# A hybrid encoder layer on one core: gelu and add of the hidden experts slot by slot in the prompt's merge, in place of pairs

## The reference, cut to what matters

```python
# the merge, for each group of tokens
gates = sigmoid(h @ w_gate + b_gate); ga, gb = split(gates)
merged = ga * (oa @ w_oa) + gb * (ob @ w_ob)
x = x + merged @ w_out
# the experts: idx and g hold 8 heads x 16 slots for each token
u, v = expert_u[idx], expert_v[idx]
act = gelu(einsum('chkd,cd->chk', u, xc))          # one dot product a slot
out = einsum('chk,chkd->cd', g * act, v)           # one scaled add a slot
```

## Time and profile before

| what | value |
|---|---|
| time, median of 3 runs | 4975.61 us (4974.44 to 4983.41) |
| the profiled execution | 4982.06 us, its span 4980.1 us |
| TensorE matmul busy | 3114.3 us, 63% of the span |
| VectorE busy | 3330.1 us, 67% |
| ScalarE busy | 1035.4 us, 21% |
| GpSimd busy | 1748.6 us, 35% |
| mean granted clock of TensorE | 0.738 of full speed |
| mean rate of all transfers | 315 GB/s |

### The profile page before, as it was taken

One profiled execution on the slowest core, in us unless ns is written; L12 is line 12 of the kernel. 1 busy time (PEld: TensorE's weight loads), 2 busy tenths in 40 slices (PEclk: granted clock), 3 DMA queues, 4 the chain that ended last, 5 costly groups with the idle time before them and its releaser, 6 DMA issues.

```text
span 4980.1 us, 72192 instructions
## 1 busy us (share of the span) xinstructions
PE 3114.3 (63%) x27052; PEld 1785.4 (36%) x27052; DVE 3330.1 (67%) x7712; ACT 1035.4 (21%) x2821; POOL 1748.6 (35%) x1393
## 2 busy tenths in 40 slices
PE   7686489885999989954545445455455454454333
PEld 6545367664777744431312212122122122121000
DVE  4426777786888845558867767667667667577554
ACT  3311111221555511111121121111111211111111
POOL 0200033224434233314444444444444444444443
PEclk9897699987999999975656656566666566665555
DMA  6142388896444386679999999999999999999998
GB/s 237 62 165 108 105 323 323 341 338 258 167 176 164 148 304 249 244 289 383 392 399 386 389 402 393 390 408 383 397 400 395 407 386 389 387 397 389 395 398 333
DMA packets 281851, 1568.76 MB, mean 315 GB/s; under 512 B 28064, under 2 KB 48032, under 8 KB 112928
## 3 DMA queue, kind: packets, MB, share of 16 engines
q0 software_dynamic: 184320, 1342.26, 68.6%
q1 hardware_dynamic: 97184, 221.90, 12.0%
HBM read 1510.52 MB, written 53.53 MB: 314 GB/s over the span
## 4 chain that ended last, share of the span: by engine, by line
DMA 31%; PE 7%; issue 7%; DVE 5%; POOL 4%; ACT 2%; another core or an unknown queue 0%; POOLq 0%; DVEq 0%; SPq 0%; ACTq 0%
DMA prompt_exp_ring<-in_experts_dram,prompt_exp_idx 28%; PE prompt_exp_acc L1966 6%; POOL prompt_exp_ring L1619 4%; DVE prompt_exp_junk L1864 3%; DMA prompt_exp_ring<-in_experts_dram,prompt_exp_idx_all 3%; ACT prompt_exp_diag L1696 2%; PE prompt_exp_qp L1927 1%; DVE prompt_exp_pos L1743 0%; DVE prompt_exp_best L1739 0%; PE prompt_exp_qp L1987 0%; DVE prompt_exp_dot L1864 0%; DMA prompt_exp_wq<-in_w_query_dram 0%; DVE prompt_exp_crest L1748 0%; DVE prompt_exp_topi L1743 0%
## 5 line engine op out<-in xcount | busy, mean ns | idle before, releaser
L1966 PE MATMUL prompt_exp_acc<-prompt_exp_ring,prompt_exp_diag 32*32 32x512 f32 x16384 | 939.8, 944 | 1400.8 <-ACT prompt_exp_diag L1696 1397.3
L1864 DVE CUSTOM_DVE_ANT_0 prompt_exp_junk<-prompt_exp_ring,prompt_exp_h_now 128x1024 bf16<-128x1024 f32 x1024 | 1244.6, 1227 | 703.3 <-DMA prompt_exp_ring<-in_experts_dram,prompt_exp_idx 661.0
L1619 POOL DMA_INDIRECT prompt_exp_ring<-in_experts_dram,prompt_exp_idx x896 | 1032.2, 1152 | 1378.0 <-PE prompt_exp_acc L1966 1212.4
L1966 PEld LDWEIGHTS prompt_exp_acc<-prompt_exp_ring,prompt_exp_diag 32*32 32x32 f32 x16384 | 169.7, 127 | 1953.7 <-issue 1951.1
L1690 ACT ACTIVATE prompt_exp_ge<-prompt_exp_dot 128x2 f32<-128x2 f32 x512 | 104.2, 203 | 2291.1 <-DVE prompt_exp_dot L1864 2291.0
L144 POOL DMA_INDIRECT bg_ring<-in_experts_dram,bg_idx x128 | 176.8, 1381 | 663.4 <-DVE bg_acc L180 363.9
L1927 PEld LDWEIGHTS prompt_exp_qp<-prompt_exp_hT,prompt_exp_wq 128*128 128x128 f32 x2048 | 309.9, 240 | 146.3 <-issue 143.2
L283 POOL DMA_INDIRECT sample_hid_ring<-in_experts_dram,sample_hid_idx x128 | 149.5, 1168 | 549.9 <-DVE sample_hid_acc L313 527.8
L1927 PE MATMUL prompt_exp_qp<-prompt_exp_hT,prompt_exp_wq 128*128 128x128 f32 x2048 | 332.9, 330 | 4.5 <-DMA prompt_exp_wq<-in_w_query_dram 2.6
L296 DVE CUSTOM_DVE_ANT_0 sample_hid_junk<-sample_hid_ring,sample_hid_h 128x1024 bf16<-128x1024 f32 x128 | 203.6, 1591 | 155.5 <-DMA sample_hid_ring<-in_experts_dram,sample_hid_idx 145.6
L703 PE MATMUL prompt_proj_acc<-prompt_proj_w_hi,prompt_proj_hT_hi 128*128 128x512 f32 x640 | 261.1, 408 | 25.7 <-ACT prompt_proj_w_hi L596 21.8
(11 more groups left out here) (349 smaller groups left out, 5050.2 us busy)
## 6 DMA issues: line engine op xcount, KB each, us to landing
sample_proj_w<-in_w_all_dram SPq DMA_DIRECT2D x10, 2048.0 KB, 9.3
prompt_proj_w<-in_w_all_dram SPq DMA_DIRECT2D x10, 2048.0 KB
proj_dram<-prompt_proj_stage SPq DMA_DIRECT2D x80, 256.0 KB
prompt_exp_ring<-in_experts_dram,prompt_exp_idx POOLq DMA_INDIRECT x896
sample_exp_wq<-in_w_query_dram SPq DMA_DIRECT2D x4, 2048.0 KB, 15.4
prompt_att_q<-proj_dram SPq DMA_DIRECT2D x16, 512.0 KB
mixed_dram<-prompt_att_OT SPq DMA_DIRECT2D x8, 1024.0 KB, 3.8
prompt_mrg_mixT<-mixed_dram SPq DMA_DIRECT2D x8, 1024.0 KB
```

What stands on the lines that cost most here:

```text
L1619: nc.gpsimd.indirect_dma_start(out=ring[:, s % RING, :], out_offset=None, in_=experts, in_offset=bass.IndirectOffsetOnAxis(ap=column(s), a ...
L1864: nc.vector.tensor_tensor_reduce(out=junk[:, s % 2, :], in0=ring[:, s % RING, 0:D], in1=h_now[:], scale=1.0, scalar=0.0, op0=ALU.mult, op1 ...
L1966: last = nc.tensor.matmul(acc[at:at + Q, rows, :], diag[k, (g - 1) % 2, c, :], ring[k, s % RING, D + half * 512:D + half * 512 + 512], sta ...
```

## The change

One number: the plan of the merge has groups of one slot in place of two. The lag stays one group.

```diff
         PLACES = 6
-        plan = Plan(first, SLOTS - first, PLACES * G, 2, 1)
+        plan = Plan(first, SLOTS - first, PLACES * G, 1, 1)
```

## The result

| | before | after |
|---|---|---|
| median of four runs | 4976.56 us (4974.44 to 4983.41) | 4946.55 us (4939.81 to 4952.47) |
| ratio | | 0.9934, 95% interval 0.9912 to 0.9955 |
| the profiled execution | 4982.06 us, span 4980.1 | 4939.81 us, span 4937.9 |
| VectorE busy | 3330.1 us | 3340.8 us |
| ScalarE busy | 1035.4 us | 1042.4 us |

The kernel is 30.0 us faster by the medians (0.66%), where 33 us and a median of 4943 were forecast. Before it ran from 1770.34 to 2145.51, 375.2 us; after, from 1767.56 to 2108.86, 341.3 us.

What follows compares the result with a forecast made beforehand. It took the merge's end as the bound, with Z idling for a late mT. Gaps of 23.3 us plus slow Z of 9.7 us gave 33 us off, a median of 4943 us; range 4936 to 4960 us.

Steps and rivals of the forecast that it cites:

- The bound: Merge: Z idles 24.5 us, mostly for mT, whose copy stands behind a gelu that waits for a gathered row.
- The cover: VectorE in the merge: 8.2 us of dots and adds between add and dot cut the 143.7 us wait to 10 to 30.
- The last gelu before the copy: ScalarE in a merge tile: third gelu ends early enough that mT has 12 us to spare; T starts the first Y.
- What is added: 32 more weight products on VectorE, 5.0 us, and 32 more gelus on ScalarE, 6.4 us, all hidden under TensorE.
- What is moved: GpSimd issues two gathers, not one, ahead of the second bias add; wo lands near 1823, nothing lost.
- The sum: Whole kernel: gaps before Z 23.3 us plus slower Z products 9.7 us, 33 us taken off.
- Slow Z: TensorE in the merge: four Z products partly at the lower clock behind longer idling; 9.7 us to win.
- The rule against it: GpSimd's bias add and VectorE's work hold a port from each other; at most 4.5 us a tile, hidden.
- (a): Rival: gaps go but Z products stay slow, 23.3 us won, 4952; chance 0.17 shared with the other partial-gain rival.
- (b): Rival: gathers still bind at some places, Z waits in half the tiles, 16 us, 4959; 0.17 shared between both partial-gain rivals.
- nothing: Rival: VectorE's loop of add, gather and dot keeps its 46.5 us a tile, 4976; chance 0.07.
- The slower one: Rival: the hand-over dot, gelu, weight, add, once a slot, stalls VectorE; 5003 at 3 us a slot; chance 0.06.

Runs made afterwards that it cites:

- pairs_copy_first: Kernel before, with the gelus of a tile's first two places behind the copy of mT in ScalarE's order; ratio 1.0006, merge 376.8 us.
- single_late: Kernel after, with each gather of the merge released one, two or three adds later; 4955.59, 4980.23 and 5215.56 us, one run each.
- single_late3: Kernel after, with each gather of the merge released three adds later, so nothing covers it; 5215.56 us, one run.
- single_late2: Kernel after, with each gather of the merge released two adds later, leaving one dot and one add as cover; 4980.23 us, one run.

## Why the prediction was right

**The bound.** Right in its cause, and one link was put too strongly. The chain "landing row, dot, gelu, copy, Z" was read as what held Z. pairs_copy_first cut it at the gelu, and TensorE waited elsewhere for as long. The better reading was in the earlier trace rows: 26.4 us of VectorE's work and 18 us of ring waits a tile (143.7 / 8) are 44.4 of its 46.5 us. That sum alone is no proof, since TensorE's work and waits fill the period as well. What decides is who waits for whom: in the merge before, VectorE waited for TensorE once, 3.9 us ahead of the last residual add, and TensorE waited 24.5 us for what hangs on VectorE. So VectorE's stalled loop was the period, and each of its products (merged, the dot for the gelu, the residual) was a way for it to reach TensorE. Of a change that moves only the copy, the text on record would have forecast 18 us and more, and this reading nothing, which is what the run gave. The forecast took no harm from it, because the change removes the stalls themselves.

**The cover.** Right. Three dots and three adds, 8.2 us bare, were to bring 143.7 us down to 10 to 30; 8.1 came. The steps of single_late show how safe that was: 5.5 us would have done as well, 2.7 not. The gathers land 5.6, 7.9 and 16.5 us after their issue at least, in the middle and at most, where the earlier trace rows has 5.7, 7.7 and 10.5, so it isn't by quicker transfers that the waits went.

**The last gelu before the copy.** Forecast: third gelu over at T + 11.9, copy over at T + 15.9, Z due at T + 28.3. With T = 1882.42 (the Z that starts at 1868.61 and 13.81 us) they are at T + 11.7, T + 15.7 and T + 28.3 (1894.08, 1898.16 and 1910.68).

**What is added.** 32 more weight products and 32 more gelus hid, as said; VectorE's tile is 26.70 us in three of five, 26.74 and 29.76 in the others, where 27.0 were worked out. The weight products took 14.5 us in all (64 of them) where 64 x 0.155 is 9.9, since four of them stand beside GpSimd's bias add and take 1.31 to 1.36 us. Adds waited for ScalarE 0.8 us, once.

**What is moved.** wo was issued at 1781.02 and landed 33.9 us later, at 1815, where I had put it near 1823; the first Z has no wait. The last residual's x was not late: stored at 2094.24, loaded from 2099.35, and the add at 2108.97 waited for Z alone. Store to load was 5.1 us, 8.0 in the earlier trace rows.

**The sum.** Gaps: 24.5 us before, 1.1 after, 23.4 where 23.3 were forecast. Slow Z: four of 15.70 to 16.93 us are now 13.90 or 14.00, 9.8 us where the forecast has 9.7. From the first Y on, the forecast put the last Z's end at 2111.5 - 1770.34 = 341.2 us; it took 341.3. That this agrees to 0.1 us is in part luck: the stretch ahead of the first Z, taken over unchanged, grew by 0.5 us (1826.53 - 1767.56 against 1828.83 - 1770.34). The medians differ by 30.0 us and not by 33; the interval, 22 to 44 us, holds both, and the experts' part alone varies by more than the difference.

**The rule against it.** The lock was met. VectorE's timeline after:

```profile
1863.94 5.53 DVE L296 CUSTOM_DVE_ANT_0 sample_hid_junk<-sample_hid_ring,sample_hid_h 128x1024 bf16<-128x1024 f32 x1
...
1904.63 1.31 DVE L305 TENSOR_TENSOR sample_hid_w<-sample_hid_ge,sample_hid_g 128x1 f32<-128x1 f32 x1
```

and GpSimd's:

```profile
1863.28 5.11 POOL L1322 TENSOR_TENSOR prompt_mrg_gate<-prompt_mrg_gate,prompt_mrg_bias 128x2048 f32<-128x2048 f32 x1 [3.98 <-DMA prompt_mrg_gate<-proj_dram]
...
1901.40 4.51 POOL L1322 TENSOR_TENSOR prompt_mrg_gate<-prompt_mrg_gate,prompt_mrg_bias 128x2048 f32<-128x2048 f32 x1
```

A dot that takes 1.22 us alone started 0.66 us behind a bias add and ended 1.1 us behind it: 4.3 us lost. A weight product that takes 0.15 us alone started within the next bias add and took 1.31 us, to its end. It is the case that the rule in the Trainium skill, SBUF — State Buffer, "Who interferes with whom", describes, and the upper bound that the forecast gave it (4.5 us a tile). The tile from 1840.54, which holds that dot, has 29.76 us of VectorE's work, in place of 26.70, and TensorE lost nothing.

**The rivals.** (a) fell: every Z behind no idling ran at 13.90. (b) and "nothing" fell with the ring's 8.1 us. The slower one fell too: even a second dot behind each one leaves the merge at 340.7 us.

## What to carry to other kernels

When rows of a ring are released by one instruction and needed by a later one on the same engine, count the engine's work between the two and hold it against the transfers' time to landing: here 2.7 us of work for each row cost 39.3 us of merge, and 2.7 us for every second row 33.9 us, while 5.5 us cost nothing, with the same ring and the same number of gathers. The 5.5 us were less than the 6.7 us that a row took to land; they were enough because VectorE had 15 us to spare in a tile, so the spare time belongs in the sum. Here dots and adds that alternate gave each row more cover than dots and adds in pairs, at no cost in memory. And before blaming the instruction that a late engine waits for, ask of each engine for whom it waits. Any engine's work and waits fill the period; the one that sets it here was the one whose waits were for its own transfers and not for the other engines. Cutting the chain behind it at one place moved the wait elsewhere.

## What was not expected of the hardware

TensorE's clock and idling. In the kernel after, the granted clock is 1.00 in every tile. In single_late3 TensorE idles 33 us before most Z products, and they take no longer than those behind 4.80 us in the earlier trace rows:

```profile
1920.72 16.89 PE L1431 MATMUL prompt_mrg_Z<-prompt_mrg_wo,prompt_mrg_mT 128*128 128x512 f32 x32 [33.22 <-ACT prompt_mrg_mT L1357]
```

```profile
1920.72:1937.61 16.89, 16.89 (x33) 7.43 (x34) 4.78 (x8) 0.20 (x1) 1.88 (x2) 0.83 0.36 120
1887.50:1920.70 33.20, 0.00 (x1) 0.00 (x0) 11.87 (x18) 6.19 (x8) 2.82 (x3) 0.57 0.50 190
```

The clock during the idle stretch is at 0.57 on the mean, over this Z at 0.83, so a part of it ran at 1.2 GHz and the rest at 2.4. Of the eight Z products there, behind 13.0 to 33.7 us of idling, seven took 16.68 to 17.02 us and one 15.58. A return from idling thus cost some 3 us of a Z at most, no more behind 33 us than behind 4.80, so that for the same idle time many such gaps cost more than one long one. How short a gap is free isn't told by its length alone: behind 3.38 us a Z took 15.70 us in the kernel before, behind 3.40 us it took 14.00 in single_late2. The granted clock was 1.00 over both idle stretches, then 0.89 over the first Z and 1.00 over the second. What decides between the two was not settled.

The gathers' times to landing overlap far more than I had reckoned: from single_late3 to single_late2, with two in flight instead of one, 388.2 us of waits fall to 130.0. The work between add and dot, 59 times 2.7 us or 159 us, accounts for a part of that; the other 99 us came with the second gather in flight.

The prompt's experts, 57% of the kernel, varied by 25 us between profiled executions of kernels that don't touch them (2806 to 2831 us). A change of 10 us in the merge is plain in its timeline and just visible in the medians.
